# Delta rule in chunks of 128 tokens instead of 64, inside a transformer block on one Trainium2 core

## The reference

```
CHUNK = 64
def chunk_gated_delta_rule(q, k, v, g, beta):
    g_cum = jnp.cumsum(g, axis=-1)                     # inside a chunk
    decay = jnp.exp(where(lower_incl, g_cum[..., :, None] - g_cum[..., None, :], -inf))
    a_mat = where(strict, einsum(k_beta, k) * decay, 0)
    m_mat = a_mat + eye(CHUNK)
    value = solve(m_mat, v_beta)
    k_cumdecay = solve(m_mat, k_beta * exp(g_cum))
    attn_intra = einsum(q, k) * decay
    def step(state, inp):                              # one chunk after the other
        v_new = val - kcd @ state
        o = qd @ state + ai @ v_new
        state = state * cd + kd.T @ v_new
        return state, o
```

## Time and profile before

| | us |
|---|---|
| timed runs, median of 3 | 2044.83 (2044.36 to 2046.23) |
| the profiled execution | 2047.77 |
| its span | 2045.7 |
| PE busy | 1998.8 (98%) |
| DVE busy | 1107.0 (54%) |
| ACT busy | 850.6 (42%) |
| POOL busy | 93.2 (5%) |

### The profile page before, as it was taken

One profiled execution on the slowest core, in us unless ns is written; L12 is line 12 of the kernel. 1 busy time (PEld: TensorE's weight loads), 2 busy tenths in 40 slices (PEclk: granted clock), 3 DMA queues, 4 the chain that ended last, 5 costly groups with the idle time before them and its releaser, 6 DMA issues.

```text
span 2045.7 us, 28100 instructions
## 1 busy us (share of the span) xinstructions
PE 1998.8 (98%) x10255; PEld 1703.2 (83%) x10255; DVE 1107.0 (54%) x1258; ACT 850.6 (42%) x953; POOL 93.2 (5%) x112
## 2 busy tenths in 40 slices
PE   9999999999999999999988999999999999999996
PEld 7888888888888879999978977788888888888885
DVE  4555455555444465776584455755554555544455
ACT  4444444444333334445554433344444444433342
POOL 0000000000000012000035210000000000000000
PEclk9999999999999999999999999999999999999998
DMA  8666666665555656655520027466666666555663
GB/s 277 188 191 188 185 181 193 194 190 189 179 180 191 240 155 206 192 162 136 170 73 1 1 91 258 135 204 187 191 187 185 180 193 194 188 170 193 198 202 123
DMA packets 186084, 355.02 MB, mean 174 GB/s; under 512 B 11200, under 2 KB 24096, under 8 KB 185264
## 3 DMA queue, kind: packets, MB, share of 16 engines
q1 hardware_dynamic: 184224, 345.29, 54.2%
q0 software_dynamic: 1696, 8.99, 1.4%
q10 hardware_dynamic: 112, 0.05, 0.0%
HBM read 352.18 MB, written 2.10 MB: 173 GB/s over the span
## 4 chain that ended last, share of the span: by engine, by line
PE 90%; DVE 5%; issue 3%; ACT 1%; POOL 0%; DMA 0%; DVEq 0%; SPq 0%; POOLq 0%; ACTq 0%
PE acc L338 25%; PE acc L340 25%; PE acc L339 25%; PE acc L349 3%; PE acc L353 3%; PE acc L351 3%; PE tp L568 1%; PE acc L1771 1%; PE tp L1762 1%; DVE wlo L319 1%; PE tp L387 1%; DVE resid L675 0%; DVE resid L470 0%; ACT whi L313 0%; PE acc L397 0%
## 5 line engine op out<-in xcount | busy, mean ns | idle before, releaser
L319 DVE TENSOR_TENSOR wlo<-raw,whi 128x1024 fp32r<-128x1024 f32 (+2 forms) x667 | 797.9, 1204 | 822.1 <-ACT whi L313 822.1
L313 ACT ACTIVATE whi<-raw 128x1024 fp32r<-128x1024 f32 (+2 forms) x667 | 689.9, 1042 | 1012.8 <-PE acc L340 933.3
L338 PE MATMUL acc<-whi,xT 128*128 128x512 f32 (+2 forms) x1724 | 663.6, 385 | 6.3 <-DVE xT L440 2.8
L340 PE MATMUL acc<-whi,xT 128*128 128x512 f32 (+2 forms) x1724 | 658.2, 382 | 0.0
L339 PE MATMUL acc<-wlo,xT 128*128 128x512 f32 (+2 forms) x1724 | 657.5, 381 | 0.0
L338 PEld LDWEIGHTS acc<-whi,xT 128*128 128x128 f32 x1724 | 324.8, 188 | 76.2 <-DVE xT L440 3.3
L340 PEld LDWEIGHTS acc<-whi,xT 128*128 128x128 f32 x1724 | 324.7, 188 | 62.6
L339 PEld LDWEIGHTS acc<-wlo,xT 128*128 128x128 f32 x1724 | 325.0, 189 | 58.3
L338 PE MATMUL acc<-whi,hT 128*128 128x512 f32 x704 | 275.3, 391 | 1.9 <-DVE resid L675 1.9
L340 PE MATMUL acc<-whi,hT 128*128 128x512 f32 x704 | 274.2, 389 | 0.0
L339 PE MATMUL acc<-wlo,hT 128*128 128x512 f32 x704 | 274.0, 389 | 0.0
(11 more groups left out here) (288 smaller groups left out, 1153.8 us busy)
## 6 DMA issues: line engine op xcount, KB each, us to landing
raw<-in_ffn_w_up_dram SPq DMA_DIRECT2D x176, 512.0 KB, 3.7
raw<-in_ffn_w_down_dram SPq DMA_DIRECT2D x176, 512.0 KB, 4.1
raw<-in_ffn_w_gate_dram SPq DMA_DIRECT2D x175, 512.0 KB, 3.8
raw<-in_w_in_dram SPq DMA_DIRECT2D x48, 512.0 KB, 3.6
raw<-in_w_out_dram SPq DMA_DIRECT2D x32, 512.0 KB, 6.2
raw<-in_w_in_dram SPq DMA_DIRECT2D x32, 260.0 KB, 2.9
raw<-in_w_in_dram SPq DMA_DIRECT2D x16, 456.0 KB, 3.9
raw<-in_w_q_idx_dram SPq DMA_DIRECT2D x8, 512.0 KB, 6.3
```

The source lines that it names most:

```text
L313: act.activation(whi[:, s, :, 0:w], raw[:, r, :, 0:w], ACT.Copy).then_inc(hi_done, 1)
L319: dve.tensor_tensor(wlo[:, s, :, 0:w], raw[:, r, :, 0:w], whi[:, s, :, 0:w].bitcast(F32), ALU.subtract).then_inc(lo_done, 1)
L338: pe.matmul(o, hi, whi[:, s, k, 0:width], start=first and k == 0, stop=False)
L340: ins = pe.matmul(o, lo, whi[:, s, k, 0:width], start=False, stop=last and k == UNIT_KT - 1)
```

## The change

A tile is one chunk. The masks lose their half blocks: `up_to`, `later` and `not_ahead` are plain triangles, `in_half` goes, and with it the two decays `cd0` and `cd1`. The scan becomes one step: tile 0 starts from a zero state, so it has only values; its state goes once into tile 1. So `kdec` is needed for tile 0 alone and `kbeg` for tile 1 alone. The inverse now needs blocks of 128: behind the 20 steps come four more, on the one 64x64 block per head below the diagonal, taken straight from `aT`.

```
-        STEPS = 4 * LEVELS
-        CHR = P // 2
+        JOIN = 4 * LEVELS
+        STEPS = JOIN + 4
+        HALF = P // 2
+        UPPER, LOWER = slice(0, HALF), slice(HALF, P)
...
         (POOL)
-                for dst, f in ((kbeg, "c2"), (kdec, "c3")):
-                    pool.tensor_tensor(group(dst, t, hh), group(ktok, t, hh), sm_group(f, t, hh), ALU.mult)
+                dst, f = ((kdec, "c3"), (kbeg, "c2"))[t]
+                pool.tensor_tensor(group(dst, t, hh), group(ktok, t, hh), sm_group(f, t, hh), ALU.mult)
...
-                if t == T - 1:
-                    z_tile(pool, t)
...
         (PE, gates)
-                    for n, m in enumerate((up_to[:], later[:], in_half[:, 0], in_half[:, 1])):
+                    for n, m in enumerate((up_to[:], later[:])):
...
         (PE, inversion, step s)
-                        ins = pe.matmul(bankF(s % 4)[:, k * P:k * P + P], lev[:, t, h], xinv[:, t, h],
-                                        start=True, stop=True)
+                        if s < JOIN:
+                            ins = pe.matmul(bankF(s % 4)[:, k * P:k * P + P], lev[:, t, h], xinv[:, t, h], ...)
+                        else:
+                            ins = pe.matmul(bankF(s % 4)[LOWER, k * HALF:k * HALF + HALF], aT[UPPER, t, h, LOWER],
+                                            xinv[UPPER, t, h, UPPER], start=True, stop=True)
...
+                            ins = pe.matmul(bankE(n)[UPPER, k * HALF:k * HALF + HALF], t1[LOWER, t, h, UPPER],
+                                            yinv[LOWER, t, h, LOWER], start=True, stop=True)
...
-                if 0 <= s - 2 < STEPS - 4:
+                if 0 <= s - 2 < JOIN:
...
+                            ins = pe.transpose(bankF(n)[UPPER, k * HALF:k * HALF + HALF],
+                                               yinv[UPPER, t, G8 * hh + k, UPPER], ident[UPPER, UPPER])
...
         (ACT: the copies of the new steps)
+                        act.activation(t1[LOWER, t, G8 * hh:G8 * hh + G8, 0:HALF], heads_half(bankF(s % 4), LOWER),
+                                       ACT.Copy).then_inc(sem("t1"), 1)
+                        act.activation(low(xinv, t, hh), heads_half(bankF((s - 2) % 4), UPPER), ACT.Copy)
...
         (DVE: the block of the inverse)
+                    dve.tensor_scalar(yinv[UPPER, t, G8 * hh:G8 * hh + G8, HALF:P], heads_half(bankE(s % 4), UPPER),
+                                      -1.0, None, ALU.mult).then_inc(sem("y_up"), 1)
...
         (ACT behind the inversion)
+            for b in range(2):
+                act.activation(vnew0[:, 4 * b:4 * b + 4, :], heads4(bankF(b)), ACT.Copy).then_inc(sem("vnew"), 1)
+            for b in range(2):
+                act.activation(nkcdT[:, 4 * b:4 * b + 4, :], heads4(bankF(2 + b)), ACT.Copy, scale=-1.0)
+            act.wait_ge(sem("o_ps"), 1)
+            act.activation(t1[:, 0], o_banks(0), ACT.Square).then_inc(sem("o_sq"), 1)
+            for b in range(2):
+                act.activation(vnew1[:, 4 * b:4 * b + 4, :], heads4(bankE(b)), ACT.Copy).then_inc(sem("vnew"), 1)
+            act.wait_ge(sem("o_sum"), 2)
+            act.activation(t1[:, 1], oy[:, 1], ACT.Square).then_inc(sem("o_sq"), 1)
...
         (PE, output projection)
-            pe.wait_ge(sem("o_sum"), O_SUMS[T - 2] + 2)
             for u in range(3):
                 out_unit(0, u)
```

More of the change, by code:

```diff
@@ L1147, in gate_exps, with o_banks, low, heads_half @@
                .then_inc(sem("gate_act"), 1)
[L1149 to L1153, removed]
[L1155 to L1167 removed]
+        def o_banks(n):
+            banks = (acc1[:], tp[:, 0:2], tp[:, 2:4])[n]
+            return banks.rearrange("p b (h c) -> p (b h) c", h=4)
+        JOIN = 4 * LEVELS
+        STEPS = JOIN + 4
+        HALF = P // 2
+        def low(tile, t, hh):
+            return tile[0:HALF, t, G8 * hh:G8 * hh + G8, 0:HALF]
+        def heads_half(bank, rows):
+            return bank[rows, 0:G8 * HALF].rearrange("p (h c) -> p h c", h=G8)
+        UPPER, LOWER = slice(0, HALF), slice(HALF, P)
         thz = thz_sb[:]
@@ new lines, in mixer_dve @@
+            for b in range(2):
+                dve.wait_ge(sem("st_ps"), b + 1)
+                dve.tensor_copy(state[:, 4 * b:4 * b + 4], heads4(bankF(2 + b))).then_inc(sem("state"), 1)
+            dve.wait_ge(sem("o_ps"), 1)
+            dve.wait_ge(sem("o_sq"), 1)
+            z_times_o(0)
+            o_mean_square(0)
+            dve.wait_ge(sem("oq_ps"), 1)
+            dve.tensor_tensor(oy[:, 1], o_banks(1), sm("eg")[:, 1].unsqueeze(2).to_broadcast([P, BH, BD]), ALU.mult)\
+               .then_inc(sem("o_sum"), 1)
@@ new lines, in mixer_pe @@
+            for h in range(BH):
+                pe.matmul(acc0[:, h // 4, head_cols(h)], yinv[:, 1, h], vb[:, 1, h],
+                          start=h % 4 == 0, stop=True, skip_group_check=True)
+            for h in range(BH):
+                if h % 4 == 0:
+                    pe.wait_ge(sem("vnew"), h // 4 + 1)
+                    pe.wait_ge(sem("nkcd"), h // 4 + 1)
+                ins = pe.matmul(tp[:, 2 + h // 4, head_cols(h)], kdec[:, 0, h], vnew0[:, h], start=True, stop=True)
+                if h % 4 == 3:
+                    ins.then_inc(sem("st_ps"), 1)
@@ new lines, in mixer_pe @@
+            for h in range(BH):
+                ins = pe.matmul(acc1[:, h // 4, head_cols(h)], aiT[:, 0, h], vnew0[:, h], start=True, stop=True)
+            ins.then_inc(sem("o_ps"), 1)
+            for h in range(BH):
+                if h % 4 == 0:
+                    pe.wait_ge(sem("state"), h // 4 + 1)
+                ins = pe.matmul(acc0[:, h // 4, head_cols(h)], nkcdT[:, h], state[:, h],
+                                start=False, stop=True, skip_group_check=True)
+                if h % 4 == 3:
+                    ins.then_inc(sem("vn_ps"), 1)
@@ L1837, in out_unit @@
+            for h in range(BH):
+                ins = pe.matmul(tp[:, h // 4, head_cols(h)], qT_of(h, 1), state[:, h], start=True, stop=True)
+            ins.then_inc(sem("oq_ps"), 1)
+            for h in range(BH):
+                if h % 4 == 0:
+                    pe.wait_ge(sem("vnew"), 2 + h // 4 + 1)
+                ins = pe.matmul(tp[:, 2 + h // 4, head_cols(h)], aiT[:, 1, h], vnew1[:, h], start=True, stop=True)
+            ins.then_inc(sem("o_ps"), 1)
             def out_unit(c, u):
```

208 lines of the change are left out of this document (70 added, 138 removed).

## The result

The changed kernel takes 2033.95 us (median of 4 runs, 2033.08 to 2034.15); the kernel before, run beside it, 2045.42 (4 runs, 2044.36 to 2046.23). The ratio is 0.9946, with a 95% interval of 0.9931 to 0.9960: faster by 0.54%, 11.5 us. Forecast were 2035.2 us and a range of 2032.5 to 2040.0.

A forecast was written before the change was run, and what follows sets the result against it. PE's own work was taken to bound the kernel. The terms -15.4 + 5.9 + 0 + 0.3 - 0.4 sum to -9.6 us, moving the median from 2044.8 to 2035.2 us, range 2032.5 to 2040.0.

The forecast's parts named there:

- Removed, -15.4: Delta-rule scan on PE: 128 records replace 240, 29.7 us become 14.3 without waits, a change of -15.4 us.
- Added, +5.9: Sixth inversion level: 80 half-price records 4.4 us, six shape changes 1.2, pipeline drain 0.3; between 4.8 and 10.2.
- The tail, 0: From last output product to PE's first transposition: 12.0 us taken, no change, between -0.4 and +1.6 us.
- upper end of my range: Tail: POOL's small steps held up behind VectorE, tail up to 13.5 us, +1.6.
- The clock, +0.3: PE's granted clock behind the longer gap at the result's transpositions: +0.3 us taken.
- allowed -1.8: Behind the longer gap at the transpositions PE could have its full clock, 1.8 us less.
- allowed +1.7: Behind the longer gap at the transpositions PE's half clock could last longer, 1.7 us more.
- The gates' sums, -0.4: Two of four PE products that sum the gates go: 4 records of 0.10 us, -0.4 us.
- Dear narrow blocks: Rival in the sixth level: half blocks cost as much as full, level 10.2 us, time 2039.5; chance 0.22.
- The tail grows: Rival: POOL's small steps stand behind VectorE, more half clock; 1.6 + 1.4 us more, time 2038.2; chance 0.15.
- exposed hand-overs: Rival in the one-step chain, or both dear blocks and grown tail: gain under 4.1 us, about 2041.5; chance 0.04.
- a clock lost in the stretch: Rival from the join to the last product: grant falls to half, 20 us more, time 2055; chance 0.02.

The follow-up runs named there:

- order of the tail: Changed kernel with VectorE scaling tile 0 and reducing tile 1 at once, split and z product while POOL works; 2031.04 us.
- power alone: Kernel of the order of the tail, with VectorE adding epsilon so that POOL keeps only the power step; 2029.39 us.
- POOL first: Changed kernel, but VectorE begins scaling tile 0 only when POOL's epsilon addition for tile 1 has ended; 2033.98 us.

## Why the prediction was right

**What bounds.** PE's own work, read from the earlier trace rows, was the right thing to look at. From the landmark to the transpositions and three products behind them PE's busy time fell by 8.7 us and the time by 10.2; between the two lie 1.3 us in which PE stood still inside the scan before (28.4 busy of 29.7) and now nowhere, and 0.2 less standstill in the tail. That the page's 11.2 lies so near the medians' 11.5 is chance, since 2.8 of it lie behind the delta rule.

**Removed, -15.4.** Measured -15.2. The 128 records have the 0.112 us of the long row, and PE waits for nothing: every copy lay beside eight products as laid out. The 0.2 us that are missing are the return from narrow to full shape at L1780 (1.98 against 1.79), which I had counted in the level.

**Added, +5.9.** Measured +5.5, and in two kernels. The choice of half a record, taken from the weight loads of the earlier trace rows against the 0.10 us of the earlier trace rows, was right: 0.058 measured, and blocks of full size cost 3.4 us more. (The eight of the earlier trace rows are eight records and so four products; the 0.10 is right as the price of a record.) The Trainium skill, "TensorE: Matmul & The Clock Gate", LDWEIGHTS, gives 53 ns for 64 columns, and the trace agrees within 5 ns. The rest of the sum came near by offsetting errors. The 80 records cost 4.6 instead of 4.4. The six changes of shape at 0.2, 1.2 in all, stand against 1.3 of another make: two returns at 0.20 (the third is the one at L1780), four turns to transpositions at 0.11 and three to narrow products at 0.14, four of these seven turns without a change of shape. The waits for copies cost 0.2 instead of 0.3. And 0.5 is saved by the products of two lines in the same time, which the sum did not have. That makes 5.6, and without the overlap it would have been 6.1.

**The tail, 0.** Measured -0.5, and two errors stand against each other in it. I had expected that VectorE's 2.6 us beside POOL would be longer than POOL's two steps of 0.24 and 1.68. The first did take 0.25, but the power step took 2.48, as it waited for VectorE's scaling (1.25 us, begun 0.3 us earlier). Only the upper end of my range had such a hold-up, with the epsilon step's row for it; it came at the power step. With the hand-overs between them POOL's two steps took 2.9 us, 0.3 more than the 2.6 that I had beside them. On the other side square, product and reduction took 0.96, 1.14 and 1.14 in the chain where I had counted 1.06, 1.22 and 1.21, and the other hand-overs 0.25 in place of 0.5. My terms add up to 11.7, and 11.5 was measured; the 12.0 that made it "no change" was a choice above the sum.

**The clock, +0.3.** Measured 0 in this stretch. PE's pause grew from 2.18 to 3.33 us, and the half clock behind it was as long as before (1.71 us lacking in both). The allowed -1.8 did occur in other kernels of this case, four of them with a pause of 1.1 to 3.3 us; the allowed +1.7 in none. So the term came near, but nothing here says when the clock falls, and on that side it is luck.

**The gates' sums, -0.4.** Measured -0.3: the row is now 0.35 us for four records instead of 0.80 for eight.

**The rivals.** "Dear narrow blocks" (0.22) fell by the 0.058 and by the full-block kernel, which at 2036.93 is less slow than the rival said: full blocks have no changes of shape to pay, 6 times 0.2 of the rival's 10.2, and 8.9 us were measured. "The tail grows" (0.15) had its mechanism half right, at the power step instead of the small one, but not its time. The range that the prediction gives its own sum, up to 2037.5, does not hold both its upper ends: +1.6 and +1.4 make 2038.2, as the second rival has it. Nothing was seen of exposed hand-overs or of a clock lost in the stretch, which stayed at 1.00 through the narrow products.

## What to carry to other kernels

On a path that is all PE, count records and price each by its weight load: a 64x64 block costs half a 128x128 one (0.058 against 0.112 us), each return to full shape 0.2 us, each turn between transpositions and narrow products 0.1, and a merge of steps that halves the serial products pays even with an inversion level added. Then look at what stands behind PE's last product: here the order of five VectorE operations was worth 2.2 us, and one 8-element step taken off POOL another 1.0. And before a gain of 1 to 3 us is believed from one profile, add up the granted clock over both: two profiles of these kernels differ by 3.4 us in it, at places whose code did not change, and whether the change had a hand in that is not shown.

## What the runs showed of the hardware

**POOL waits for the VectorE operation under way, and only for that one.** The undisturbed steps take 0.24 and 1.68 us. Beside an operation of VectorE with two operands in SBUF that had begun before, they took longer by about what it had left, counted to 1.14 us behind its start, when the next operation of VectorE could begin: 0.84 left, 2.48 for 1.68 (changed kernel); 0.96 left, 1.16 for 0.24 (order of the tail, addition); 0.87 left, 2.49 for 1.68 (the same, power); 0.97 left, 2.54 for 1.68 (power alone). The sums would be 2.52, 1.20, 2.55 and 2.65. In the last case VectorE began another such operation while the power step ran, and neither lasted longer for it. With POOL first, 1.67 (one run). Beside VectorE's L1518, which reads one operand from PSUM, POOL's steps for tile 0 took their 0.24 and 1.68 in the changed kernel, though the first began 0.18 us behind it. POOL's product of 1024 columns did hold up VectorE's split, 1.50 instead of 1.23. The Trainium skill, "GPSIMD Engine Reference", section Specifications, says that POOL shares its way to SBUF with VectorE and that two SBUF inputs of VectorE bring contention; the trace agrees, with these numbers.

**The clock falls in equal steps that a kernel mostly repeats.** Each fall lacks 1.70 to 1.71 us or twice that. Behind the second norm all three profiles of the kernel before have one, and of the ten of other versions only that with POOL first. The changed kernel shows the same pattern twice, the kernel before nearly the same three times, but the better order of the tail differs from the changed kernel at the start (1.70 against 0), over 1100 us ahead of its edit. Ahead of the transpositions it fell behind pauses of 2.18 (kernel before, three times), 3.31, 3.32 and 3.33 us, and not behind 1.15, 2.13, 2.46 and 3.32 in four other kernels; with POOL first (3.23) it fell only within the second eight. So the length of the pause alone does not decide it; what does stays open.

Not tried: a split of unit 2 further ahead, for which ACT is idle 4.23 us before its last square; and a fourth unit of the output projection in the gap.
